# Query statistics and decode heads in column groups of 32, state-space sums partly in PSUM, responses in two banks

## The reference, cut to what matters

```python
def swa_prompt(h, ...):                      # 16 query heads, 4 key heads, 64 wide
    q, k, v = qkv_project(h, w_qkv, q_gain, k_gain)   # q and k are normed per head
    scores = einsum(q, [previous block, own block] of k) * 64 ** -0.5
    o = softmax([scores where valid, sink])[..., :-1] @ v
    return o @ w_o
def swa_sample(h, cache_k, cache_v, ...):    # 8 samples, 128 cached keys each
    kk, vv = [cache, new] ; o = the same with the window's last 128 keys

def s5_mixer(h, ...):                        # 64 groups of 16 channels, 64 complex states
    bu = einsum('nlgc,gpc->nlgp', u, bb)     # complex
    x_t = ab * x_{t-1} + bu_t                # a scan over the positions
    y = Re(x @ c) + d_skip * h ; z = gelu(y)
    zz = z @ w_glu ; out = zz[:D] * sigmoid(zz[D:])

for i in range(2):
    x = x + mixer_i(rmsnorm(x)) ; x = x + conv_ffn(rmsnorm(x))
```

## Time and profile before

| | us |
|---|---|
| median of 3 runs (1148.19 to 1150.76) | 1149.44 |
| the execution that was profiled | 1153.15 |
| its span in the trace | 1151.4 |
| PE busy in it | 1118.7 (97%) |
| DVE, ACT, POOL busy | 721.3, 455.0, 424.7 |

### The profile page before, as it was taken

One profiled execution on the slowest core, in us unless ns is written; L12 is line 12 of the kernel. 1 busy time (PEld: TensorE's weight loads), 2 busy tenths in 40 slices (PEclk: granted clock), 3 DMA queues, 4 the chain that ended last, 5 costly groups with the idle time before them and its releaser, 6 DMA issues. The chain is left out here.

```text
span 1151.4 us, 25215 instructions
## 1 busy us (share of the span) xinstructions
PE 1118.7 (97%) x9760; PEld 1096.1 (95%) x9760; DVE 721.3 (63%) x1132; ACT 455.0 (40%) x752; POOL 424.7 (37%) x688
## 2 busy tenths in 40 slices
PE   5999899999999999999998899999999999999998
PEld 5999789999999999999997899999999999999998
DVE  5874756688885248887337945557776424777622
ACT  5324763454442134443444333335444213444410
POOL 6012106999999899991247830000000000000000
PEclk9998989999999999999999999999999999999999
DMA  7422002333353323354746432222223322222322
GB/s 240 153 74 66 1 1 79 130 122 128 109 213 119 106 92 109 109 182 146 254 128 201 146 96 91 91 78 87 91 91 105 102 87 73 91 91 91 119 90 99
DMA packets 47703, 129.05 MB, mean 112 GB/s; under 512 B 12064, under 2 KB 17424, under 8 KB 47648
## 3 DMA queue, kind: packets, MB, share of 16 engines
q1 hardware_dynamic: 42272, 114.68, 30.2%
q0 software_dynamic: 5376, 13.63, 3.6%
HBM read 109.79 MB, written 18.21 MB: 111 GB/s over the span
## 5 line engine op out<-in xcount | busy, mean ns | idle before, releaser
L1584 PE MATMUL ps<-hx_hi,w_hi 128*128 128x260 f32 x1600 | 456.5, 285 | 16.5 <-DVE w_lo L1061 11.8
L1586 PE MATMUL ps<-hx_hi,w_lo 128*128 128x260 f32 x1600 | 454.0, 284 | 0.0
L1585 PE MATMUL ps<-hx_lo,w_hi 128*128 128x260 f32 x1600 | 452.7, 283 | 0.0
L754 ACT ACTIVATE w_hi<-w_raw 128x1024 fp32r<-128x1024 f32 (+1 forms) x156 | 175.7, 1126 | 441.8 <-PE ps L1586 441.7
L1584 PEld LDWEIGHTS ps<-hx_hi,w_hi 128*128 128x128 f32 x1600 | 303.0, 189 | 19.5 <-DVE w_lo L1061 12.0
L1585 PEld LDWEIGHTS ps<-hx_lo,w_hi 128*128 128x128 f32 x1600 | 303.0, 189 | 0.1
L1586 PEld LDWEIGHTS ps<-hx_hi,w_lo 128*128 128x128 f32 x1600 | 303.1, 189 | 0.0
L1061 DVE TENSOR_TENSOR w_lo<-w_raw,w_hi 128x1024 fp32r<-128x1024 f32 (+1 forms) x156 | 208.9, 1339 | 92.6 <-ACT w_hi L754 91.9
L1584 PE MATMUL ps<-hid_hi,w_hi 128*128 128x260 f32 x704 | 199.1, 283 | 0.2 <-DVE hid_lo L1406 0.2
L1586 PE MATMUL ps<-hid_hi,w_lo 128*128 128x260 f32 x704 | 198.7, 282 | 0.0
L1585 PE MATMUL ps<-hid_lo,w_hi 128*128 128x260 f32 x704 | 198.7, 282 | 0.0
(11 more groups left out here) (285 smaller groups left out, 1610.0 us busy)
## 6 DMA issues: line engine op xcount, KB each, us to landing
w_raw<-in_wup SPq DMA_DIRECT2D x88, 512.0 KB, 3.3
w_raw<-in_wdn SPq DMA_DIRECT2D x32, 704.0 KB, 4.1
w_raw<-in_wglu SPq DMA_DIRECT2D x16, 512.0 KB, 3.3
w_raw<-in_wqkv SPq DMA_DIRECT2D x12, 512.0 KB, 3.4
w_raw<-in_wo SPq DMA_DIRECT2D x8, 512.0 KB, 3.3
g_scr<-rec POOLq DMA_DIRECT2D x8, 512.0 KB, 3.1
c_scr<-rec POOLq DMA_DIRECT2D x8, 512.0 KB, 3.0
wst<-g_scr SPq DMA_DIRECT2D x8, 512.0 KB, 8.0
```

The source lines that it names most:

```text
L754: act.activation(w_hi[b][:, 0:kt * P], w_raw[b][:, 0:kt * P], ACT.Copy).then_inc(hi_done, 1)
L1584: pe.matmul(out, wh, xh, start=(k == 0), stop=False)
L1585: pe.matmul(out, wh, xl, start=False, stop=False)
L1586: ins = pe.matmul(out, wl, xh, start=False, stop=(k == kt - 1))
```

## The change

- **Query statistics.** `query_stat(t)` goes. `stats(r)` takes the tiles in three groups, (0,1), (2,3,4,5), (6,7). For each tile it is one product: the weights are 32 columns of the matrix of head means, the moving side 512 columns of squares, and tile m of the group writes the partitions 32m to 32m+31 of bank 7. ACT copies the bank (`stat_out`), PE turns it (`turn_stats`, four transposes), DVE copies 16 or 32 columns out of it. `stats` stands behind the units 6 and 10 and behind `sample_stat`, `turn_stats` behind the units 7 and 11 and behind `scores(2, 0)`; `query_copy(1)` stands at unit 11 on DVE instead of 10, `query_copy(2)` behind the first half of the masking of pair 2 instead of ahead of it, and `reciprocals(0)` waits for it. On POOL both halves of the padded queries and their memset (512 columns instead of 128) stand ahead of the second `query_rstd`.
- **Samples.** The queries lie padded in blocks of 32 columns; they are the weights, the 128 keys are the moving side, and four products write four groups of 32 partitions at a time, added over four rounds so that a row is a head of a sample. Heads are now on partitions, `sample_turn(0)` is gone, and `sample_max`, `sample_exp` and `sample_norm` stand one pair earlier. `sample_values` is cut in four and stands before turn(5), (6), (7) and (8); a piece is 8 products of 64-column weights with 4 moving columns.
- **State-space sums.** DVE makes v0*e0 and v1*e0 in SBUF, multiplies v0 and v1 by e1 in place in PSUM, and the sum and the difference read one operand from SBUF and one from PSUM. Six instructions stay six; three waits between them instead of four.
- **Responses.** The second four go to bank 7 and are turned there, each half into its own bank; two waits go. `states_in(2)` and `turn_responses(1)` stand ahead of `table_outputs(0)`.
- **u by tile.** DVE and POOL wait for the DMAs of the tile that they scale instead of those of all tiles. In the last tile of the third norm ACT squares before it writes its two copies.

The core of the difference:

```diff
+        GROUP = ((0, 1), (2, 3, 4, 5), (6, 7))
-            query_rstd(0, 0, 16)
-            pair_queries(0)
-            query_rstd(1, 16, 48)
-            pair_queries(1)
-            query_rstd(2, 48, 65)
+            after(pool.memset(q_rs[:, 65:66], -0.5))
+            query_rstd(0, 16, 1)
+            pool.wait_ge(sem("ks_turned"), 2)
+            after(pool.memset(q_pad[:], 0.0))
+            pad_queries(0)
+            pad_queries(1)
+            query_rstd(16, 48, 2)
+            sample_rstd()
+            query_rstd(48, 64, 4)
...
+            def stats(r):
+                pe.wait_ge(sem("qk_sq"), 3 + GROUP[r][-1])
...
+                else:
+                    pe.wait_ge(sem("q_copied"), r)
+                for m, t in enumerate(GROUP[r]):
+                    ins = pe.matmul(ps[32 * m:32 * m + 32, 7, :], head_mean[:, 48:80], query_sq(t)[:, 0:SEQ],
+                                    start=True, stop=True)
+                ins.then_inc(sem("qk_stat"), 1)
+            def turn_stats(r):
+                pe.wait_ge(sem("stat_out"), r + 1)
+                n = 32 * len(GROUP[r])
                 for blk in range(NB):
+                    ins = pe.transpose(ps[:, 7, blk * n:blk * n + n], stat_sb[r][0:n, blk * P:(blk + 1) * P],
+                                       ident[0:n, 0:n])
+                ins.then_inc(sem("stat_turned"), 1)
...
+            def sample_scores():
...
+                for b in range(4):
+                    for a in range(4):
+                        m, c0 = 4 * a + b, a * P + 24 * b
+                        ins = pe.matmul(ps[32 * a:32 * a + 32, 6, 256:384], q_pad[:, c0:c0 + 32],
+                                        ksT[:, m * P:(m + 1) * P], start=(b == 0), stop=(b == 3),
...
                 if j == 0:
-                    pe.wait_ge(sem("s_st_done"), 1)
+                    pe.wait_ge(sem("q_copied"), 4)
...
-                tt(vt[0], v[0][:, :, 0:NC], e[0], ALU.mult)
-                after(tt(vt[1], v[1][:, :, 0:NC], e[1], ALU.mult))
-                after(tt(vr[0], vt[0], vt[1], ALU.add))
-                tt(vt[0], v[1][:, :, 0:NC], e[0], ALU.mult)
-                after(tt(vt[1], v[0][:, :, 0:NC], e[1], ALU.mult))
-                after(tt(vr[1], vt[0], vt[1], ALU.subtract))
+                v0, v1 = v[0][:, :, 0:NC], v[1][:, :, 0:NC]
+                tt(vt[0], v0, e[0], ALU.mult)
+                after(tt(vt[1], v1, e[0], ALU.mult))
+                tt(v0, v0, e[1], ALU.mult)
+                after(tt(v1, v1, e[1], ALU.mult))
+                tt(vr[0], vt[0], v1, ALU.add)
+                after(tt(vr[1], vt[1], v0, ALU.subtract))
...
-                if j == 4:
-                    pe.wait_ge(sem("resp_out"), 1)
...
-                if h == 1:
-                    pe.wait_ge(sem("rsb_full"), 1)
...
+            states_in(2)
+            turn_responses(1)
             table_outputs(0)
-            turn_responses(1)
-            states_in(2)
             state_outputs(0)
```

More of the change, by code:

```diff
@@ L131, in trunk_program @@
         qn_sq, _ = place("qn_sq", P, at=TMP + 5632)
-        q_pair, _ = place("q_pair", P, at=TMP + 4608)
+        q_pad, _ = place("q_pad", 2 * NS * 32, at=TMP + 6144)
+        sq_of = [place("sq_q4", TOK, at=D0)[0], place("sq_q5", TOK, at=D0 + 2080)[0]]
+        stat_sb = [place(f"stat_sb{r}", SEQ, at=D0 + (10240, 4160, 4160)[r])[0] for r in range(3)]
         q_st, _ = place("q_st", 65, at=D1 + 38272)
@@ L596, in pair_queries, with rstd_of @@
[L596 to L601, removed]
+            def rstd_of(lo, hi):
+                after(pool.tensor_scalar(q_st[:, lo:hi], q_st[:, lo:hi], EPS, None, ALU.add))
+                return pool.tensor_tensor(q_rs[:, lo:hi], q_st[:, lo:hi],
+                                          q_rs[:, 65:66].to_broadcast([P, hi - lo]), ALU.pow)
@@ new lines, in query_rstd, with sample_rstd @@
+            def query_rstd(lo, hi, copied):
+                pool.wait_ge(sem("q_copied"), copied)
+                after(rstd_of(lo, hi))
+                after(pool.tensor_scalar(nq_rms[:, lo:hi], q_rs[:, lo:hi], -SCALE, None, ALU.mult))
+                pool.sem_inc(sem("q_rstd"), 1)
+            def sample_rstd():
+                pool.wait_ge(sem("q_copied"), 3)
+                after(pool.tensor_scalar(q_st[:, 64:65], q_st[:, 64:65], float(D // HD), None, ALU.mult))
+                after(rstd_of(64, 65))
+                after(pool.tensor_scalar(s_soft[:, 6:7], q_rs[:, 64:65], SCALE, None, ALU.mult))
+                after(pool.tensor_scalar(s_soft[:, 7:8], q_rs[:, 64:65], -SCALE, None, ALU.mult))
+                pool.sem_inc(sem("s_rstd"), 1)
@@ L773, in norm_in @@
                                    ACT.Copy, scale=g).then_inc(sem("h_done"), 1)
-                    act.activation(sq[b][:], tiles(x, k), ACT.Square).then_inc(sq_done, 1)
+                    if not last:
+                        act.activation(sq[b][:], tiles(x, k), ACT.Square).then_inc(sq_done, 1)
             def norm_sd(n):
@@ L1363, in _ @@
                 if j == 0:
-                    query_copy(2)
+                    sample_copy()
                 if j + 2 < NPR:
@@ L1744, in _ @@
                     values_turn()
-                elif u >= 5:
-                    query_stat(u - 5)
-                if u == 11:
-                    sample_scores(0)
+                elif u in (6, 10):
+                    stats(u // 10)
+                elif u in (7, 11):
+                    turn_stats(u // 11)
                 if u in (6, 7):
@@ L1830, in _ @@
             turn(0)
-            query_stat(7)
-            sample_scores(1)
+            sample_scores()
             sample_stat()
+            stats(2)
             for j in range(NPR):
@@ L1838, in _ @@
                     scores(j + 2, 0)
+                if j == 0:
+                    turn_stats(2)
                 turn(2 * j + 1)
```

170 lines of the change are left out of this document (82 added, 88 removed).

## The result

| | before | after |
|---|---|---|
| median, us | 1148.97 | 1138.34 |
| lowest to highest of 4 | 1148.19 to 1150.76 | 1138.17 to 1139.99 |
| execution that was profiled | 1153.15 | 1138.17 |
| its span | 1151.4 | 1136.4 |
| its mean granted clock | 0.989 | 0.997 |

The ratio is 0.9914 (95% interval 0.9888 to 0.9940): about 10 us faster. The forecast was 1131.6 with a range up to 1137.5, so the direction was right and the gain was forecast too large, 17.8 against 10.6. In the two profiled executions the difference is 15.0.

What follows compares the result with a forecast made beforehand. PE, busy 97% of the span, was taken as the bound. Gains of 2.6 (statistics), 7.0 (attention) and 8.2 (state-space) sum to 17.8 us: 1135.35 profiled, 1131.6 median; own range 1129 to 1134, with rivals 1127.5 to 1137.5.

Steps and rivals of the forecast that it cites:

- The step from the profiled execution to the median: End of the sum: 17.8 us off the profiled 1153.15 gives 1135.35; median 3.7 lower, so 1131.6.
- Statistics among the units: Before T, the end of unit 11: three statistics calls replace six, added copies hidden beside dense products; gain 2.6 us.
- Start and rest of the attention: From T to wo: gains 4.5 and 4.7 us, less 1.7 for a clock fall and 0.5 for hand-overs: 7.0.
- Up to the first outputs: State-space stage before its loop: two waits go and table_outputs(0) runs at full clock; gain 4.6 us.
- SP issues `toep` earlier by both, 1.65, and it lands at 622.5: Ahead of the state-space loop: two removed waits, 0.40 and 1.27 us, let toep be issued and land earlier.
- Loop: State-space loop: PE sets a period of 5.5 to 5.6, gain 3.5; ah wait 0.85 goes; 0.75 off for gelu.
- Rival (b): State-space sums stay slow, the loop gains only 0.4 us; total gain 13.9, 1135.5 us; chance 0.18.
- That frees 2 x 0.45 us per period: State-space loop: DVE's two sums fall to 0.42 us each, freeing 0.9 a period, over PE's 0.46 wait.
- (d): Column groups do not overlap: statistics take 1.5, 3.1 and 1.5 us, sample scores 3.1; 1136 to 1138; chance 0.04.
- (e): Slower than before: the clock falls at the idle before reciprocals(0) and stays low through attention; near 1160 us; chance 0.03.
- (a): Attention: clock falls again or stays low longer, a further 6.8 us at half clock; gain 14.4, 1135 us; chance 0.16.
- (c): Attention: no clock fall at all and a shorter wait at reciprocals(0); gain 19.7, 1129.7 us; chance 0.15.

Runs made afterwards that it cites:

- mask_first: Changed kernel with DVE's masking of pair 0 ahead of the seven operations on the samples' states at unit 8; 1137.23 us (0.9902).
- rstd_split: Changed kernel with POOL's power of tile 2 (8 columns) ahead of and apart from that of tiles 3 to 5; 1133.88 us (0.9879).
- resp_u_only: Kernel before with only responses in two banks, u by tile, early last square and PE's new order; 1147.05 us (0.9997).
- old_square: Changed kernel with ACT's last square of the third norm behind its two copies again, as before; 1137.28 us (0.9903).
- toep_first: Changed kernel with glu's second-unit weights and the first record block moved behind toep transfers on SP; 1137.41 us (0.9908).
- the repaired kernel: Not defined by this name; fits the changed kernel with rstd_split, mask_first and old_square together: 1132.05 us (0.9858).
- attn_only: Kernel before with only the change's query statistics and samples' heads, no state-space part; 1142.84 us (0.9955).

## Why the prediction was wrong

**The step from the profiled execution to the median.** "1135.35. The median of before is 3.7 lower, ... so 1131.6 for the median." This is the largest miss. The sum took the 23.9 us at half clock of one execution, a loss of some 12, as the kernel's own, and subtracted all of it but 1.7. That execution lay above every one of the 62 executions of before that were timed beside the experiments (1143.18 to 1152.99). The middle one of the 27 in the first group ran at a mean clock of 0.993 instead of 0.989, which by the line above is 3.7 us. Measured against 1153.15 the change gained 15.0; against the median 10.6: 4.4 of the 7.2 that are missing. The other 2.8 are in the terms below. The trace offered this before the run: its 1153.15 lay outside the three timed runs.

**Statistics among the units: 2.6, measured 1.3.** The prices were right: 1.0 for either group and 0.4 for the turn, 2.4 in place of the six calls' 5.1, so 2.7 saved. The sentence that failed is "hidden", which I asked of the added work only. What the removed statistics had covered was DVE's first masking, queued behind 3 us of states: 1.04 of new wait, shown by `mask_first`. The last 0.3 is spread over hand-overs of 0.1 between the units.

**Start and rest of the attention: 7.0, measured 7.1.** Turn(2) came at T+17.4, forecast 15.0 and 1.7 for the fall; from there 51.4, forecast 51.7. The chain over the power on 32 columns, the wait of 3.7 and the fall behind it came as told, and `rstd_split` shows wait and fall to be one thing. But the 7.1 is the difference to an execution with 20.5 us at half clock here. `resp_u_only`, with the attention code of before and 3.4 us at half clock, took 68.4 where the changed kernel took 68.8: the term is mostly clock, and it is here that the step above bites.

**Up to the first outputs: 4.6, measured 2.1** (0.6 ahead of L1594 and 1.5 behind). The step "SP issues `toep` earlier by both, 1.65, and it lands at 622.5" took the old landing time for one transfer among fewer. Counted from L1594, PE could use it 20.7 behind, where it was 18.9 before and 17.7 in the forecast. And "ACT squares before its copies" left out what stands behind the copies: the store, then SP's whole queue. `old_square` gives back 2.5, `toep_first` 1.9. The 1.16 of `states_in(2)` for the last table's copy was in the code and I did not price it. PE's order itself is worth 1.0 to 1.2 in the traces.

**Loop: 3.5 + 0.85 - 0.75, measured 4.4.** Period 5.55, forecast 5.5 to 5.6; sums 0.42, products written to PSUM 0.42 to 0.43. Rival (b) is out. "That frees 2 x 0.45 us per period" was half right: the rotation gave 1.07 and the scans took 0.50 back. It was enough, since DVE's 5.42 still lies under PE's 5.55.

Of the rivals, (d) and (e) did not come, nor (a) in the profiled execution; one of the four ran at a mean clock of 0.994 and took 1.7 us more, where no trace was taken; (c) is what the typical execution of the repaired kernel does. The Trainium skill ("SBUF — State Buffer", SBUF: two separate sides) says that a DVE operation with two SBUF inputs and a GpSimd operation that reads SBUF exclude each other for a whole instruction. This case's traces agree: sums with both inputs in SBUF took 424 ns beside an idle POOL and 840 to 982 beside a busy one, and the sums with one input in PSUM 421 beside a busy one. Freed of POOL at the sums, DVE meets it at the next such instruction. The rule of the Trainium skill ("TensorE: Matmul & The Clock Gate", Part 4: PE-mode transpose) that transposes do not count as busy time for the clock is neither shown nor refuted here. Most falls seen follow a wait (3.71, 2.36, 2.08) or narrow products; the one at 599.8 in `attn_only` has a wait of 0.40 and four records of 8 columns ahead of it, then transposes and responses, and other traces have the same rows at full clock.

## What to carry to other kernels

Read the clock of several executions before half-clock stretches of one profile go into a sum, and price them by the middle one. When work is taken off the critical engine, ask what it covered on the other engines, and when a transfer is issued earlier, what it is issued into. A collision between two engines that is removed at one instruction can come back at the next with the same operands.

## What was not expected of the hardware

- Executions of one and the same kernel differed by 8.8 us in one group of runs (1143.18 to 1152.01), and the mean clock (0.998 to 0.989) goes with it at a correlation of 0.95. The stretches at half clock between T and the end of the loop lasted 3.4, 6.8 or 13.7 us in all traces.
- With a row of 32 narrow records, 3.6 us long and without a wait, the clock was below 1.0 in five of six executions; with the same values in narrower weights and four pieces of 0.5 to 0.6 it stayed at 1.0 in three of four. No trace shows the fall itself.
- DVE's product in place in PSUM took 432 and 423 ns, 8 to 11 ns more than from PSUM to SBUF (424 and 412).
- POOL's power took 5.45 us on 32 columns, 4.18 on 24, 2.93 on 16, 1.67 on 8 and 0.58 on one: some 0.16 a column. Splitting off the 8 columns that were needed first was worth 4.5 us.
